# A store moved behind weight fetches, and blocks of outputs moved behind transposed parts, in the last phase of a hybrid attention layer

## The reference, cut to what matters

```
h    = rmsnorm(x);  proj = h @ w_in                   # q, k, v of both groups, q of memory, gates
sb   = stick_breaking_attention(...)                  # 8 heads
fx   = forgetting_attention(...)                      # 8 heads, softmax with forget gates
m    = memory_attention(...)                          # 4 heads over 256 memory rows
y    = concat(sb, fx, m)                              # 1280 columns, 20 heads of 64
y    = rmsnorm per head of y * out_norm_w * silu(gate)
x    = x + y @ w_out
out  = rmsnorm(x)
```

## Time and profile before

| | |
|---|---|
| median of three runs | 793.46 us (793.13 to 793.98) |
| the profiled execution | 793.03 us, span 791.1 us |
| mean granted clock of TensorE | 0.998 of full speed |
| PE busy | 776.6 us, 98% of the span |
| DVE, ACT, POOL busy | 605.0, 445.7, 257.7 us (76, 56, 33%) |
| chain that ended last | PE 85%, DVE 7%, DMA 2%, ACT 2%, issue 2% |

### The profile page before, as it was taken

One profiled execution on the slowest core, in us unless ns is written; L12 is line 12 of the kernel. 1 busy time (PEld: TensorE's weight loads), 2 busy tenths in 40 slices (PEclk: granted clock), 3 DMA queues, 4 the chain that ended last, 5 costly groups with the idle time before them and its releaser, 6 DMA issues.

```text
span 791.1 us, 11916 instructions
## 1 busy us (share of the span) xinstructions
PE 776.6 (98%) x4030; PEld 653.2 (83%) x4030; DVE 605.0 (76%) x1206; ACT 445.7 (56%) x920; POOL 257.7 (33%) x440
## 2 busy tenths in 40 slices
PE   8999999999999999999999999999999999999997
PEld 8878887888888888888888888888888887878775
DVE  6877687776789777768977777898767688685676
ACT  7767765556646555665745667465555574542232
POOL 1112733242156326223823521383234124210000
PEclk9999999999999999999999999999999999999999
DMA  9413824124113412521261142106213398233523
GB/s 355 134 63 141 278 98 148 54 69 106 67 54 98 144 40 69 134 67 54 65 175 41 68 125 77 54 27 178 76 55 81 110 386 300 82 107 107 187 96 143
DMA packets 37708, 93.25 MB, mean 118 GB/s; under 512 B 5000, under 2 KB 13192, under 8 KB 36624
## 3 DMA queue, kind: packets, MB, share of 16 engines
q1 hardware_dynamic: 37648, 92.50, 36.1%
HBM read 61.91 MB, written 21.66 MB: 106 GB/s over the span
## 4 chain that ended last, share of the span: by engine, by line
PE 85%; DVE 7%; DMA 2%; ACT 2%; issue 2%; SPq 0%; POOL 0%; ACTq 0%; DVEq 0%; POOLq 0%
PE banks L867 16%; PE banks L869 15%; PE banks L868 15%; PE banks L1037 8%; PE banks L912 8%; PE banks L1057 5%; PE banks L1024 4%; PE banks L1056 4%; PE banks L1023 4%; PE banks L1108 1%; DMA hT<-wo_dram 1%; PE banks L984 1%; DMA work<-part_dram 1%; PE banks L1077 1%; DVE pT L1876 1%
## 5 line engine op out<-in xcount | busy, mean ns | idle before, releaser
L867 PE MATMUL banks<-hT,w_parts 128*128 128x512 f32 x576 | 237.6, 412 | 0.3 <-DVE sb_heads L1735 0.2
L869 PE MATMUL banks<-hT,w_parts 128*128 128x512 f32 x576 | 225.8, 392 | 0.0
L868 PE MATMUL banks<-hT,w_parts 128*128 128x512 f32 x576 | 225.4, 391 | 0.0
L1266 ACT ACTIVATE pT<-banks 128x512 fp32r<-128x512 f32 x208 | 92.4, 497 | 126.7 <-PE banks L1037 126.4
L1876 DVE TENSOR_TENSOR pT<-banks,pT 128x512 fp32r<-128x512 f32 x208 | 108.4, 563 | 66.6 <-ACT pT L1266 65.3
L869 PEld LDWEIGHTS banks<-hT,w_parts 128*128 128x128 f32 x576 | 108.1, 188 | 24.5
L867 PEld LDWEIGHTS banks<-hT,w_parts 128*128 128x128 f32 x576 | 108.5, 188 | 15.8 <-DVE sb_heads L1735 1.0
L868 PEld LDWEIGHTS banks<-hT,w_parts 128*128 128x128 f32 x576 | 109.0, 189 | 13.6
L1534 POOL TENSOR_TENSOR w_parts<-w_raw,w_parts 128x1024 fp32r<-128x1024 f32 x34 | 81.4, 2395 | 91.9 <-ACT w_parts L1165 91.9
L1541 POOL TENSOR_SCALAR_AFFINE_SELECT work<-work 128x128 f32<-128x128 f32 x64 | 30.4, 475 | 192.7 <-ACT work L1243 192.7
L1836 DVE TENSOR_TENSOR_SCAN work<-work 128x639 f32<-128x639 f32 (+3 forms) x64 | 90.7, 1418 | 0.7 <-POOL work L1541 0.6
(11 more groups left out here) (258 smaller groups left out, 1355.9 us busy)
## 6 DMA issues: line engine op xcount, KB each, us to landing
w_raw<-in_w_tiles SPq DMA_DIRECT2D x36, 512.0 KB, 3.9
hT<-wo_dram SPq DMA_DIRECT2D x14, 512.0 KB, 8.4
fx_heads<-fx_heads SPq DMA_DIRECT2D x8, 512.0 KB, 7.8
negL<-negL_dram SPq DMA_DIRECT2D x8, 512.0 KB, 6.1
yT_dram<-silu SPq DMA_DIRECT2D x8, 512.0 KB, 4.1
sb_heads<-sb_heads SPq DMA_DIRECT2D x8, 512.0 KB, 6.7
negL<-yT_dram SPq DMA_DIRECT2D x8, 512.0 KB, 4.9
work<-in_x SPq DMA_DIRECT2D x6, 512.0 KB, 6.7
```

Source lines behind the costliest of these rows:

```text
L867: pe.matmul(o, w[0][:, k, :], hT[:, 0, k, tok], start=(k == 0), stop=False)
L868: pe.matmul(o, w[0][:, k, :], hT[:, 1, k, tok], start=False, stop=False)
L869: mm = pe.matmul(o, w[1][:, k, :], hT[:, 0, k, tok], start=False, stop=(k == KT - 1))
L1266: act.activation(pT[:, n % 3, 0, cols], banks[:, T_BANK + n % 2, cols], ACT.Copy).then_inc(t_hi, 1)
```

## The change

On SP the store of the last gates goes from ahead of the fetches of weight blocks 6 to 9 to behind them. On ACT `y_hi` goes from the head of a tick to behind its transposed parts and small pieces. On DVE `y_lo` goes likewise behind them, and the turn and product of the last scales (an "N3" piece of the last phase) go ahead of `output` in their tick.

```diff
             fetch_w_out(0)
-            sp.wait_ge(piece_done, piece_of("G", 1, LAST) + 1)
-            sp.dma_start(silu_dram[:, :], gate_of(LAST)).then_inc(silu_out, 16)
             sp.wait_ge(piece_ready, piece_of("G", 1, LAST - 1) + 1)
             for j in range(6, NB):
                 fetch_w_out(j)
             for j in range(NB, NT_OUT):
                 fetch_w_out(j)
+            sp.wait_ge(piece_done, piece_of("G", 1, LAST) + 1)
+            sp.dma_start(silu_dram[:, :], gate_of(LAST)).then_inc(silu_out, 16)
             load_x(1)
...
                     sigmoids(i)
-                for n in Y_AT[i]:
-                    y_hi(n)
...
                         y_end_hi(SMALL[n].of - LAST + 1, SMALL[n].c)
+                for n in Y_AT[i]:
+                    y_hi(n)
...
                     turn_scales(ph)
-                for n in Y_AT[i]:
-                    y_lo(n)
+                ended = [n for n in SMALL_AT[i] if (SMALL[n].what, SMALL[n].of) == ("N3", LAST)]
+                for n in ended:
+                    finish_small(n)
                 if i in OUT_AT:
                     output(OUT_AT[i])
...
                 for n in SMALL_AT[i]:
-                    if n not in early:
+                    if n not in early + ended:
                         finish_small(n)
                     if SMALL[n].what == "N3" and SMALL[n].of == LAST:
                         y_end_lo(1, SMALL[n].c)
...
                         y_end_lo(0, SMALL[n].c)
+                for n in Y_AT[i]:
+                    y_lo(n)
```

## The result

The kernel after takes **795.76 us** (median of 18 runs, 794.81 to 797.44), the kernel before 793.58 us in the same batch (18 runs, 792.62 to 795.39). The ratio is **1.0026 [1.0019, 1.0034]**: slower, by 2.2 us (0.3%), which is clear of the spread of the runs. The profiled execution took 795.45 us with a span of 793.5 us, 2.4 more than before, and a mean granted clock of 0.994 (before 0.998).

The account below looks back on a forecast made before the run. TensorE was taken as the bound, with 3.6 us of waits after 600 us. Terms -1.3 - 1.1 + 2.2 = -0.2, and +1.2 for the clock, took 793.03 to 794.0; 0.4 to the median gave 794.4, range 791.8 to 796.0.

Parts of the forecast that it names:

- the likeliest case: The clock falls in the gap ahead of the fourth `end_outputs`: 794.4 us (793.9 to 795.3), chance 0.42.
- four rivals: Clock holds (0.25), fetches gain nothing (0.15), tail absorbs `y_lo(6)` (0.10), the change does less than it says (0.04).
- the fetches gain nothing: Rival: block 7's landing is set by its own issue and read rate, so 1.3 us stay; 795.7 us, chance 0.15.
- less than it says: Rival: no wait goes and `y_lo(6)` is late nonetheless; 795.7 us and more, chance 0.04.
- Part 1, -1.3: Store behind the fetches: block 7 lands 1.3 us earlier, ending TensorE's wait on `wo_dram`; bounds 0 and -1.31.
- The cover named for y(2): Block 2 of y comes 2 us later; `y_hi(2)` behind `upper_part` hides it: cost 0, without cover up to 2 us.
- Part 2 in the loop, -1.1: Tick 157, y blocks behind transposed parts: TensorE's wait for `pT` near 704 goes; bounds 0 and -1.11.
- The tail, +2.2: Tick 165: `y_lo(6)` ends 2.2 us later, delaying `load_part`, `end_sum` and the fourth `end_outputs`; bounds 0 and +2.2.
- The clock, +1.2: A 3.4 us gap ahead of the fourth `end_outputs` halves TensorE's clock, costing 1.2 us; bounds 0 and +1.95.
- was up until then: Reason for the clock's cost below 1.95 us: full clock until it falls just before or after the restart.
- lies beyond: The 3.4 us gap exceeds the 2.0 us of idleness after which the clock fell at the kernel's end.
- the clock holds: Rival: TensorE's clock stays at full level through the gap; 793.2 us, chance 0.25.

Follow-up runs that it names:

- e4: The kernel after with 18 matmuls that nobody reads put ahead of the fourth `end_outputs` on TensorE; 793.81 us.
- e2: The kernel after with `y_hi(6)` and `y_lo(6)` back at their old place, ahead of the scales' turn; 791.38 us.
- e3: The kernel after with the four `load_part` moved ahead of `load_y(7)` in SP's order; 789.46 us.
- e8: e3 with the store of the gates back ahead of the fetches of blocks 6 to 9; 790.03 us.
- e11: e3 run once more, unchanged, beside its variants; 789.07 us.
- e6: The kernel before with the store behind the fetches and block 2 of y behind the transposed parts; 792.54 us.
- e3b: The kernel before with the four `load_part` ahead of `load_y(7)`, without the change; 793.44 us.
- e1: The kernel before with only the store moved behind the fetches of blocks 6 to 9; 794.36 us.
- e7: The kernel before with the gates' store issued twice, the second into a spare tensor that nobody reads; 795.77 us.
- e5: The kernel after with GpSimd's last product (group 39) made to wait for `y_lo(6)`; 795.29 us.

## Why the prediction was right, and where its sizes were off

**Right: the mechanism of the likeliest case.** The loop gives time, the tail takes it back through `y_lo(6)`, a gap opens ahead of the fourth `end_outputs`, and the clock falls. e4 shows the clock (gap filled, 1.95 us back), e2 and e3 the order behind the gap. All four rivals are out by the rows after; that 795.7 stood beside two of them ("the fetches gain nothing", "less than it says") is chance. The likeliest case's own range, 793.9 to 795.3, missed 795.76; the wider range took it in only because it left room for those rivals.

**Part 1, -1.3.** The wait on `wo_dram` went. The store landed at 664.1 (663.6 predicted), y(2) at 669.5 (669.0). Its worth is 1.0 (e8 against e11) to 1.3 (e6 against before). Block 7's last transfer took 8.7 us from issue to landing before and 7.5 after; issued at 650.23, it landed near 657.8, where 657.7 was predicted. It took 8.6 to 9.4 us in the three kernels with one store ahead (before, e8, e3b) and 7.2 to 7.8 in nine with the store behind. But e1, the tenth with it behind, has 8.7, and e7's second store, at 9.3, made nothing later than in e3b. So that part 1 gains, once block 2 is out of its way, is shown by the time of e6 and the wait in e8; that the store's bytes are the reason isn't shown. The cover named for y(2) was needed: without it, 1.0 us (e1), where up to 2 was said.

**Part 2 in the loop, -1.1.** The wait at 704 is gone, and TensorE came to that place 2.5 us earlier (2.4 predicted for both parts).

**The tail, +2.2: mis-sized, by a neighbour that was not looked at.** `y_lo(6)` was to end at 736.1 (738.5 less the loop's 2.4). It ended at 736.66 because it took 2.03 us beside GpSimd's product (e5: 1.23 apart). The order of ACT and VectorE had been followed, and GpSimd's not: before, the product ran when VectorE was at the scales' turn, which writes a PSUM bank that the multiplication behind it reads, and neither was slowed (1.29 and 0.71 us). The first part then released VectorE at 743.91, 0.7 later than was predicted (743.37 - 0.2), and the fourth `end_outputs` started at 752.71, not 752.0. The gap was 4.5 us instead of 3.4 for this 0.7, and because TensorE came 3.6 us earlier, not 3.2.

The Trainium skill, "SBUF — State Buffer", section "Who interferes with whom", says that a VectorE instruction with two SBUF inputs contends with a GpSimd instruction that reads SBUF, and one with at most one SBUF input, outside the two-port modes, doesn't. The trace agrees: `y_lo(6)` (`negL` and `fx_heads`) went from 1.23 to 2.03 us beside the product, the product from 1.29 to 1.73 beside `y_end_lo` (`silu` and `sb_heads`), and the turn, which has one SBUF input, kept its 0.71 us beside the same product.

**The clock, +1.2: mis-sized, and its fall in part luck.** It cost 1.95 to 2.0 us. The bound from the kernel's start, 1.95, came out as the number, and the reason for going below it ("was up until then") didn't hold: at half clock from the restart at 752.71 to 757.1, nearly all of the twelve matmuls ran slow. In e5 and e2, where the clock fell only behind the restart, the same twelve took 4.40 and 4.46 us, 1.6 more than before. So the reason describes e5 and e2, and not the kernel after.

That a gap of 3.4 us "lies beyond" was argued from one row: 2.0 us from the last matmul to the fall, at the end of one execution. The same time at the end of the fourteen profiled executions is 2.0 to 4.9 us, and above 3.4 in eight of them; the 2.0 is the shortest. After the last matmul ahead of the gap it took 2.1 us in the kernel after, 2.8 in e2 and 5.0 in e5, and in the profiled execution of e7 a gap of 2.5 us passed without a fall. By these numbers a gap of 3.4 us need not have made the clock fall, and "the clock holds" was a nearer rival than its 0.25. The measured gap was 1.1 us longer than predicted, and with it the clock fell in all 18 runs (mean clock 0.994 to 0.996).

The Trainium skill's rule that the prediction cites, in "TensorE: Matmul & The Clock Gate", section "Why this matters for your kernels", agrees with the gaps of 4.5 and 3.9 us. The rows of e2 and e7 (1.8 us with a fall, 2.5 without) show that the length of a gap alone doesn't decide it below that.

**The sum.** 0.7 (the tail) and 0.8 (the clock) are the 1.4 us by which 795.76 lies above 794.4, to within 0.1. Both go against the change. So the steps that were off are two terms of the sum: the tail's +2.2, by a VectorE instruction that took 2.03 and not 1.23 us, and the clock's +1.2, which was 1.95 to 2.0. With the clock taken at its row from the start (+1.95) the forecast would have been 795.2, and most of the chance would have stood on slower, where 0.22 stood, instead of on no change, where 0.64 did. The prediction named the transfer behind `y_lo(6)` as the whole of the loss; mending its place in SP's order is worth 6.3 us in the kernel after (e3) and 0.4 in the kernel before (e3b).

## What to carry to other kernels

When a change frees the bottleneck engine, follow it to the next thing that doesn't come sooner: here 3.6 us arrived at a transfer that was queued behind another load, putting block 6 back (e2) turned 2.2 us of that into time, and moving the transfer itself (e3) 4.2 to 4.6. A gap on TensorE can be paid twice: by its own length, and by 1.6 to 2.0 us for the clock (here, by the mean clock, in every run of the kernels with gaps of 3.9 and 4.5 us, and in three of twelve of the one with 1.8), so a change that gathers small waits into one long one can lose though their sum is the same. When an instruction is moved, look at what runs beside its new place on all engines, GpSimd's too. A delay that is read from one execution, as the 2.0 us to the clock's fall, can be the shortest of many: read it in several before a forecast hangs on it.

## What of the hardware was not expected

- The time from TensorE's last matmul to the clock's fall varies much: 2.0 to 4.9 us at the ends of the fourteen profiled executions, 2.1 us in the gap of the kernel after.
- The clock can fall after TensorE has started again: 1.0 us after the restart in e2, whose gap was 1.8 us, and 1.1 us in e5, whose gap was 3.9. In the profiled execution of e7 it didn't fall for a gap of 2.5 us.
- A VectorE instruction with two SBUF inputs and GpSimd's product make the later one of the two longer: `y_lo(6)`, started 0.8 us behind the product, by 0.8 us (1.23 to 2.03); the product, started 0.1 us behind `y_end_lo`, by 0.44 us (1.29 to 1.73), while `y_end_lo` kept its 0.69 us.
